# Attention with V as the stationary operand, two query blocks at a time, and outputs written feature-major

## What is computed

```python
def odd_mixer(h, w_qkv, ..., subln, w_o, rel_table, layer_idx):
    q, k, v = jnp.split(h @ w_qkv, 3, axis=-1)      # q, k: (b, s, H, 2, 64); v: (b, s, H, 128)
    ...
    def block(args):                                 # one block of 128 queries, all heads
        bias = rel_table[t5_bucket(kpos[None, :] - qpos[:, None])]
        sc = jnp.einsum('bqhmd,bkhmd->bhmqk', qi, k) * scale + bias[None, :, None]
        p = jax.nn.softmax(sc, axis=-1)
        a = p[:, :, 0] - lam * p[:, :, 1]
        return jnp.einsum('bhqk,bkhe->bqhe', a, v)
    ...
    o = rmsnorm(o, subln) * (1.0 - lam_init)
    return o.reshape(bsz, s, H * 2 * dh) @ w_o
```

## Time and profile before

| what | value |
|---|---|
| median of 3 runs | 2960.14 us (2956.94 to 2962.92) |
| the profiled execution, its own time | 2964.82 us |
| span of the profiled execution | 2963.0 us |
| TensorE busy | 2863.3 us, 97% |
| VectorE busy | 1922.0 us, 65% |
| ScalarE busy | 1197.6 us, 40% |
| attention, from the first scores of block 0 to the output projection | about 570 us of the span, 1578 to 2149 |

### The profile page before, as it was taken

The page is one execution under the profiler, slowest core; times in us unless marked ns, Lnnn a source line. Parts: engine busy times, 40 slices in busy tenths (PEclk is TensorE's granted clock), DMA queues, the critical chain, the costliest instruction groups (busy, mean ns, idle before and its releaser), DMA issues.

```text
span 2963.0 us, 34631 instructions
## 1 busy us (share of the span) xinstructions
PE 2863.3 (97%) x13481; PEld 2263.8 (76%) x13481; DVE 1922.0 (65%) x2488; ACT 1197.6 (40%) x1932; POOL 440.0 (15%) x322
## 2 busy tenths in 40 slices
PE   8999999999999999999998999999799999999999
PEld 6767776767768888877766888888676888887887
DVE  6548775655587666765667767766726966666254
ACT  2223327413243333433245565556624433334252
POOL 0420011261003222211000000000000222222010
PEclk7999999999999999999999999999899999999999
DMA  6334474016232222385550111111123222226453
GB/s 214 115 129 148 158 212 187 15 64 220 58 114 86 86 86 82 117 252 169 165 179 15 36 43 47 52 43 43 65 92 107 86 86 79 86 71 188 144 157 116
DMA packets 361688, 326.61 MB, mean 110 GB/s; under 512 B 11502, under 2 KB 319183, under 8 KB 361487
## 3 DMA queue, kind: packets, MB, share of 16 engines
q1 hardware_dynamic: 348486, 271.61, 29.4%
q0 software_dynamic: 12000, 48.61, 4.4%
q10 hardware_dynamic: 1040, 4.19, 0.4%
HBM read 263.88 MB, written 68.35 MB: 112 GB/s over the span
## 4 chain that ended last, share of the span: by engine, by line
PE 87%; DVE 7%; ACT 2%; DMA 2%; issue 1%; POOL 1%; SPq 0%; ACTq 0%; DVEq 0%; POOLq 0%
PE psum_gemm L1932 20%; PE psum_misc L1932 17%; PE psum_gemm L2378 8%; PE psum_gemm L216 6%; PE psum_gemm L217 6%; PE psum_gemm L220 6%; PE psum_misc L2442 3%; PE psum_gemm L2463 3%; PE psum_gemm L2451 3%; PE psum_misc L216 2%; PE psum_misc L217 2%; PE psum_misc L220 2%; DVE mix_out L285 1%; PE psum_gemm L318 1%; PE psum_misc L888 1%
## 5 line engine op out<-in xcount | busy, mean ns | idle before, releaser
L216 PE MATMUL psum_gemm<-h_hi,w_hi 128*128 128x512 f32 x816 | 330.3, 405 | 11.4 <-DVE h_lo L401 7.6
L217 PE MATMUL psum_gemm<-h_lo,w_hi 128*128 128x512 f32 x816 | 319.2, 391 | 0.0
L198 ACT ACTIVATE w_hi<-w_raw 128x1024 fp32r<-128x1024 f32 x93 | 97.8, 1055 | 453.8 <-PE psum_gemm L220 321.2
L1857 DVE TENSOR_TENSOR ring_lo<-piece_raw,ring_hi 128x512 fp32r<-128x512 f32 x192 | 136.0, 716 | 211.8 <-ACT ring_hi L1851 211.2
L220 PE MATMUL psum_gemm<-h_hi,w_lo 128*128 128x512 f32 x816 | 252.3, 390 | 0.0
L203 DVE TENSOR_TENSOR w_lo<-w_raw,w_hi 128x1024 fp32r<-128x1024 f32 x93 | 119.1, 1285 | 158.0 <-ACT w_hi L198 158.0
L1851 ACT ACTIVATE ring_hi<-piece_raw 128x512 fp32r<-128x512 f32 x192 | 112.7, 592 | 254.3 <-PE psum_misc L1932 213.8
L1932 PE MATMUL psum_misc<-h_hi,ring_hi 128*128 128x512 f32 x512 | 200.7, 392 | 1.2 <-DVE ring_lo L1857 1.1
L216 PEld LDWEIGHTS psum_gemm<-h_hi,w_hi 128*128 128x128 f32 x816 | 153.7, 188 | 61.5 <-issue 20.7
L1932 PE MATMUL psum_misc<-h_hi,ring_lo 128*128 128x512 f32 x512 | 199.4, 389 | 0.0
L1932 PE MATMUL psum_misc<-h_lo,ring_hi 128*128 128x512 f32 x512 | 199.2, 389 | 0.0
(11 more groups left out here) (415 smaller groups left out, 6830.9 us busy)
## 6 DMA issues: line engine op xcount, KB each, us to landing
ada_w<-in_w_ada SPq DMA_DIRECT2D x28, 1024.0 KB, 5.6
w_raw<-in_f_w_up SPq DMA_DIRECT2D x52, 512.0 KB, 4.8
ffn_act_scratch<-gate_act SPq DMA_DIRECT2D x42, 512.0 KB, 2.6
piece_raw<-in_f_w_down SPq DMA_DIRECT2D x80, 256.0 KB, 3.1
piece_raw<-ffn_act_scratch SPq DMA_DIRECT2D x80, 256.0 KB, 2.9
pair_raw<-in_f_w_up SPq DMA_DIRECT2D x36, 512.0 KB, 5.1
w_raw<-in_e_w_in SPq DMA_DIRECT2D x29, 512.0 KB, 4.6
x_scratch<-x_res SPq DMA_DIRECT2D x3, 4096.0 KB, 12.5
```

The lines of the kernel that those rows point to most:

```text
L198: act.activation(w_hi[:, s], w_raw[:, s], ACT.Copy).then_inc(s_hi, 1)
L216: pe.matmul(o, wh, rh[:, k, c], start=(k == 0), stop=False)
L217: pe.matmul(o, wh, rl[:, k, c], start=False, stop=False)
L1857: dve.tensor_tensor(Al[:, idx % 7, 0:n], src, Ah[:, idx % 7, 0:n].bitcast(F32), ALU.subtract).then_inc(s_wl, 1)
```

## The change

- Operands of the product with V change places. V is stationary and the map is moving; two query blocks stand side by side in `att_T`, so that one `av(p)` serves blocks 2p and 2p+1: per 128 keys three products of 256 columns (V hi with map hi, V hi with map lo, V lo with map hi). The output is feature-major, 128 features x 256 queries, and needs no transpose; `o_step`, `o_sum`, `o_part`, GpSimd's multiplication and the transposes ahead of the last head's part of the output projection go.
- Since the queries are now along the columns, a factor per query can't be applied while copying out. ScalarE scales the first map by one over its sum ahead of the combination (`scale`), VectorE computes the factors ahead of that (`factors`), and `combine` is left with the weighted sum.
- The sum of squares over the features is a product of the squares with a matrix of ones (`square_sums`, TensorE, 256 columns), between ScalarE's `o_evac` (copy and square) and `sums_copy`.
- The norm of a head works on 128 x 1024 numbers: a square root on ScalarE (`o_std`), and on VectorE a reciprocal and a multiplication (`o_norm`, at position 2 of the next head).
- The order: `av(p)` stands in even iterations between scores and transposes, `square_sums` in odd ones behind the transposes. The projections are dealt out as 12 in even and 24 in odd iterations, all at the iteration's end; at position 0, six of the 12 stand ahead of the transposes. A group's end is no longer put ahead of `av`.

```diff
--- before.py
+++ after.py
-            lo, hi = min(max(QM * (g + 1), 0), 144 * (ATT_HEADS - 1)), min(max(QM * (g + 2), 0), 144 * (ATT_HEADS - 1))
+            lo, hi = (min(36 * (i // 2) + 24 * (i % 2), 144 * (ATT_HEADS - 1)) for i in (g + 1, g + 2))
             cut = hi // 24 * 24
             return (lo, cut, hi, True) if cut > lo else (lo, hi, hi, False)
...
-                h, i = g // CH, g % 2
-                pe.wait_ge(s_aTl, g + 1)
+            def av(p):
+                h = p // QPAIRS
+                pe.wait_ge(s_aTl, 2 * p + 2)
                 pe.wait_ge(s_vl, h + 1)
-                if g >= 1:
-                    pe.wait_ge(s_on, g)
-                o = pG[:, 0, 256 * i:256 * i + 256]
+                if p >= 1:
+                    pe.wait_ge(s_omc, p)
                 for c in range(CH):
-                    pe.matmul(o, aT[:, i, 0, c], v_hl[:, h % 2, c], start=(c == 0), stop=False, skip_group_check=True)
-                    mm = pe.matmul(o[:, 0:P], aT[:, i, 1, c], v_hl[:, h % 2, c, 0], start=False, stop=(c == CH - 1),
-                                   skip_group_check=True)
+                    for x, (v, a) in enumerate(((0, 0), (0, 1), (1, 0))):
+                        mm = pe.matmul(pG[:, 0, 0:256], v_hl[:, h % 2, c, v], aT[:, a, c].rearrange("p s q -> p (s q)"),
+                                       start=(c == 0 and x == 0), stop=(c == CH - 1 and x == 2), skip_group_check=True)
                 mm.then_inc(s_av, 1)
+
+            def square_sums(p):
+                pe.wait_ge(s_on, p + 1)
+                if p >= 1:
+                    pe.wait_ge(s_omc, p)
+                pe.matmul(pG[:, 0, 256:512], ones[:], o_sq[:], start=True, stop=True, skip_group_check=True
+                          ).then_inc(s_oms, 1)
 
             def v_step(h):
...
@@ -2486,20 +2485,22 @@
                 lo, cut, hi, at_end = qkv_range(g)
                 if 0 <= g < NB - 2:
                     scores(g + 2)
+                if g >= 2 and g % 2 == 0:
+                    av(g // 2 - 1)
                 if g >= 0:
+                    if g % CH == 0 and g:
+                        first = min(lo + 6, hi)
+                        piece(lo, first)
+                        lo = first
                     pe.wait_ge(s_a, g + 1)
                     step(lambda c: E0[:, g % 3, c * P:(c + 1) * P], s_aT, s_aTl, g + 1)
-                if at_end:
-                    piece(lo, cut)
-                    lo = cut
-                if g >= 1:
-                    av(g - 1)
+                if g >= 3 and g % 2:
+                    square_sums((g - 3) // 2)
                 piece(lo, hi)
                 if g >= 0 and g % CH == CH - 1 and g + 1 < NB:
                     v_step((g + 1) // CH)
-                if g >= CH and g % CH == O_STEP:
-                    o_step(g // CH - 1)
-            av(NB - 1)
+            av(NQPAIR - 1)
+            square_sums(NQPAIR - 1)
 
         def att_act(act):
...
                                    ).then_inc(s_pe, 1)
 
+            def scale(g):
+                act.wait_ge(s_r, 2 * g + 2)
+                act.activation(E0[:, g % 3], E0[:, g % 3], ACT.Copy, scale=inv[:, g % 8, 0:1]).then_inc(s_asc, 1)
+
             def a_hi(g):
                 act.wait_ge(s_aT, g + 1)
                 if g >= 2:
-                    act.wait_ge(s_av, g - 1)
...
-                act.activation(junk[:], o_t[:, h % 2, b], ACT.Square, accum_out=o_ss[:, h % 2, b:b + 1]).then_inc(s_osq, 1)
+                    act.wait_ge(s_av, g // 2)
+                act.activation(aT[:, 0, :, g % 2], pG[:, 1].rearrange("p (c q) -> p c q", c=CH), ACT.Copy).then_inc(s_aTh, 1)
+
+            def o_evac(p):
+                h, i = p // QPAIRS, p % QPAIRS
+                act.wait_ge(s_av, p + 1)
+                if h and i == 0:
+                    act.wait_ge(s_of, h)
+                act.activation(o_f[:, 256 * i:256 * i + 256], pG[:, 0, 0:256], ACT.Copy)
+                if p >= 1:
+                    act.wait_ge(s_oms, p)
+                act.activation(o_sq[:], pG[:, 0, 0:256], ACT.Square).then_inc(s_on, 1)
+
+            def sums_copy(p):
+                h, i = p // QPAIRS, p % QPAIRS
+                act.wait_ge(s_oms, p + 1)
+                if h and i == 0:
+                    act.wait_ge(s_os, 16 * h)
+                act.activation(r_t[:, 256 * i:256 * i + 256], pG[:, 0, 256:512], ACT.Copy).then_inc(s_omc, 1)
 
             def o_std(h):
-                act.wait_ge(s_osq, CH * (h + 1))
-                act.activation(o_sd[:, h % 2], o_ss[:, h % 2], ACT.Sqrt, bias=eps[:, 0:1], scale=1.0 / P).then_inc(s_osd, 1)
+                act.wait_ge(s_omc, QPAIRS * (h + 1))
+                act.activation(r_t[:], r_t[:], ACT.Sqrt, bias=eps[:, 0:1], scale=1.0 / P).then_inc(s_osd, 1)
 
...
             probs(0)
             v_hi(0)
             probs(1)
+            scale(0)
             for g in range(-1, NB):
                 e = ended(g)
+                if 0 <= g < NB - 1:
+                    scale(g + 1)
                 if g >= 0:
                     a_hi(g)
                 if e and e[1] < 2:
                     kq_hi(*e)
                 elif e:
                     v_copy(e[0], e[2])
-                if g >= 2:
-                    o_square(g - 2)
-                if g >= 1:
-                    o_part(g - 1)
                 if 0 <= g < NB - 2:
                     probs(g + 2)
+                if g >= 2 and g % 2 == 0:
+                    o_evac(g // 2 - 1)
+                if g >= 3 and g % 2:
+                    sums_copy((g - 3) // 2)
                 if e and e[2]:
                     next_w(U_ATT + 3 * e[0] + e[1] + 2)
                 if g >= 0 and g % CH == CH - 1 and g + 1 < NB:
                     v_hi((g + 1) // CH)
-                if g >= CH and g % CH == O_STD:
+                if g > CH and g % CH == 1:
                     o_std(g // CH - 1)
-                if g >= CH and g % CH == O_STEP:
-                    o_copy(g // CH - 1)
                 if g > NB - CH:
                     o_hi(act, g - NB + CH - 1)
-            o_square(NB - 2)
-            o_part(NB - 1)
-            o_square(NB - 1)
...
+            def factors(g):
                 s8 = g % 8
                 dve.wait_ge(s_pe, 2 * g + 2)
                 dve.reciprocal(inv[:, s8], sums[:, s8]).then_inc(s_r, 1)
                 dve.wait_ge(s_r, 2 * g + 1)
-                dve.scalar_tensor_tensor(ratio[:, s8, 0:1], sums[:, s8, 0:1], nlam[:, 0:1], inv[:, s8, 1:2], ALU.mult,
-                                         ALU.mult).then_inc(s_r, 1)
-                dve.wait_ge(s_r, 2 * g + 2)
-                dve.scalar_tensor_tensor(E0[:, g % 3], E1[:, g % 2], ratio[:, s8, 0:1], E0[:, g % 3], ALU.mult, ALU.add
+                dve.tensor_tensor(ratio[:, s8, 0:1], nlam[:, 0:1], inv[:, s8, 1:2], ALU.mult).then_inc(s_r, 1)
+
+            def combine(g):
+                dve.wait_ge(s_asc, g + 1)
+                dve.scalar_tensor_tensor(E0[:, g % 3], E1[:, g % 2], ratio[:, g % 8, 0:1], E0[:, g % 3], ALU.mult, ALU.add
                                          ).then_inc(s_a, 1)
...
+            def o_norm(h):
                 dve.wait_ge(s_osd, h + 1)
-                dve.reciprocal(o_rs[:, h % 2], o_sd[:, h % 2]).then_inc(s_ors, 1)
+                dve.reciprocal(r_t[:], r_t[:]).then_inc(s_ors, 1)
+                dve.wait_ge(s_ors, h + 1)
+                dve.scalar_tensor_tensor(r_t[:], o_f[:], nlam[:, 4:5], r_t[:], ALU.mult, ALU.mult).then_inc(s_of, 1)
...
                 e = ended(g)
+                if 0 <= g < NB - 1:
+                    factors(g + 1)
...
                     combine(g + 1)
-                if g >= 1:
-                    o_sum(g - 1)
                 if e and e[2]:
                     split_lo(dve, U_ATT + 3 * e[0] + e[1] + 2)
                 if g >= 0 and g % CH == CH - 1 and g + 1 < NB:
                     v_lo((g + 1) // CH)
-                if g >= CH and g % CH == O_STD:
-                    o_rstd(g // CH - 1)
+                if g > CH and g % CH == 2:
+                    o_norm(g // CH - 1)
```

86 lines of the change are left out of this document (23 added, 63 removed).

## The result

| | before | after |
|---|---|---|
| median of the runs | 2958.5 us (2955.6 to 2962.9) | 3065.2 us (3063.5 to 3076.0) |
| profiled execution's span | 2963.0 us | 3061.8 us |
| mean granted clock in it | 0.982 | 0.972 |

The ratio is 1.0368, 95% interval 1.0355 to 1.0381: 3.7% slower. The forecast of 3063 is 2 us off.

A forecast was written before the change was run, and what follows sets the result against it. TensorE's queue bounds seven heads, a loop through VectorE and ScalarE the last. Six heads at 13.9 (83), the first 5, the last 15: 103 us on 2964.8 gives 3068, less 4.7 is 3063; its own range 3030 to 3095, overall 2990 to 3095.

The forecast's parts named there:

- a: Positions 1 and 5: the next group waits for the shared bank's copy, 1.6 for k, 0.9 for v; 2.5 us.
- b: Position 4: `av` waits for `sums_copy` of position 3, behind the copy and `probs`; 2.0 us.
- c: Position 7: `square_sums` waits for `o_evac`, behind the copy and `probs` of position 6; 1.5 us.
- d: Position 3: the transposes wait for `combine`, behind the low part in VectorE's queue; 1.2 us.
- e: Positions 0 and 1: `av` waits 0.7 for `sums_copy`, the transposes of position 1 wait 0.8 for `combine`; 1.5 us.
- f: Position 3: `square_sums`, ahead of 24 projections, waits for `o_evac`, which waits for `o_norm` (reciprocal 6.6 us); 8.0 us.
- g: TensorE at 1.2 GHz for a while behind the long wait of f; 1.7 us, from 0 to twice that.
- TensorE's queue: Saving per head from fewer products with V, no output transposes, fewer changes of form and V's split covered; 4.5 us.
- Rival 3: The reciprocal runs at VectorE's other rate, 1.3 us, so f is 2.7 and g 0; 3010 us; chance 0.08.
- rival 4: Only the large wait counts, the small ones are covered by unseen slack; 2997 us; chance 0.15.
- Rival 5: `scale` isn't hidden on ScalarE, or 1.2 GHz costs more after 8 us; 3090 us and above; chance 0.11.
- rival 2: TensorE's queue alone decides, each of seven heads gains 4.5 us; 2929 us; chance 0.04.

The follow-up runs named there:

- small: Changed kernel, output and sums copied earlier on ScalarE, `combine` ahead of the low part, groups of positions 1 and 5 ahead of the transposes: 3020.6 us.
- final2: `final` with VectorE's `o_lo` one iteration later in the last head's blocks: 2948.1 us, ratio 0.9962 to before.
- lnexp: Changed kernel with VectorE's reciprocal replaced by a logarithm and an exponential on ScalarE in place of the root, orders unchanged: 3006.5 us.
- final: `small` with the edit of `lnexp`, `o_evac` early at every position and `o_norm` ahead of the low part of the transposed map: 2954.3 us.
- no_recip: Changed kernel with VectorE's reciprocal of 128x1024 left out, so the output differs: 3009.1 us, ratio 1.0169 to before.
- act_order: Changed kernel with `o_evac` (but at position 2) and `sums_copy` ahead of the group's copy and `probs` on ScalarE: 3050.5 us.
- sq_late: Changed kernel with the product with ones behind the 24 projections of its iteration, reciprocal kept: 3032.1 us, ratio 1.0246 to before.

## Why the prediction was right, step by step

Per head, forecast and then what the trace of after shows:

| | forecast | measured |
|---|---|---|
| a | 2.5 | (9.0 + 4.1) / 6 = 2.2 |
| b | 2.0 | 1.7 |
| c | 1.5 | 0.9 |
| d | 1.2 | 1.0 |
| e | 1.5 | 0.8 + 0.6 = 1.4 |
| f | 8.0 | 7.4 |
| g | 1.7 | 2.1 |
| TensorE's queue | -4.5 | -2.2, by difference |
| sum | 13.9 | 14.5 |

The rows for b, c and e, TensorE in order of time:

```profile
1707.06 3.11 PE L2460 MATMUL psum_gemm<-att_T,v_split 128*128 128x256 f32 x24 [1.72 <-ACT o_factor_T L2555]
...
1735.10 0.70 PE L2468 MATMUL psum_gemm<-o_squares,ones 128*128 128x256 f32 x2 [0.88 <-ACT o_squares L2548]
```
```profile
1744.60 3.11 PE L2460 MATMUL psum_gemm<-att_T,v_split 128*128 128x256 f32 x24 [0.81 <-ACT o_factor_T L2555]
...
1753.55 1.09 PE L2448 MATMUL psum_gemm<-ident,probs_a 128*128 128x128 f32 x8 [0.61 <-DVE probs_a L2644]
```

**What was right for its reason.** Each wait came at the place, for the tile and for the engine that the three queues had given. All but g are somewhat shorter than worked out, by 0.1 to 0.6 us. One reason is in the trace: the two operations of `o_evac` took 0.66 us together (1781.05 to 1781.71) where 0.9 was counted. The reciprocal took 6.547 us where 6.56 was worked out from its two narrower rows. Rival 3 hung on it and fell with that row, rival 4 on the walk through the queues, and fell with `small`, which took a to e away and gave 7.8 us a head. Rival 5 is out for the six heads: g came to 2.1, within its bounds, and no wait in them is outside a to f. Against rival 2 the forecast said that a reciprocal alone on any row costs more than 0.9 us; the row of 8 columns has 0.2. What holds is that every rate it considered gives more than 0.9 at 1024 columns. Had I gone by the reading of the Trainium skill's page "VectorE: DVE Perf Modes" (section on the fixed hardware budget) as eight cycles a column, f would have been 10.0 by that estimate; the measured 6.25 ns are six cycles at 0.96 GHz, and the rows were the better guide.

**What was mis-sized: TensorE's saving.** I had put 4.5 us and the head shows about 2.2. This is the term of the sum that was wrong. One `av` of after, and what follows it:

```profile
1724.83 3.14 PE L2460 MATMUL psum_gemm<-att_T,v_split 128*128 128x256 f32 x24
1727.81 1.04 PE L2448 MATMUL psum_gemm<-ident,probs_a 128*128 128x128 f32 x8
```

24 start to start take 2.98 us, 0.124 each and not 0.115, four times a head 0.9 us. Half the price of 512 columns was too low: eight transposes of 128 columns take 0.85 us, 0.106 each, 256 columns 0.124 and 512 columns 0.229, so the price isn't in proportion to the columns. The product with ones costs 0.49 and not 0.24:

```profile
1715.31 1.09 PE L2448 MATMUL psum_gemm<-ident,probs_a 128*128 128x128 f32 x8
1716.24 0.60 PE L2468 MATMUL psum_gemm<-o_squares,ones 128*128 128x256 f32 x2
1716.49 0.58 PE L2375 MATMUL psum_gemm<-h_hi,w_hi 128*128 128x512 f32 x1
1716.90 0.40 PE L2375 MATMUL psum_gemm<-h_lo,w_hi 128*128 128x512 f32 x1
```

From the transposes' start to the second projection's is 1.59 us, and 1.10 where no such product stands between (1711.11 - 1710.01 in the same trace). The trace holds two records for each of these products, whose operands the kernel keeps as fp32 and not as fp32r like those of its other products. I had halved the interval of the earlier trace rows as two products, and 0.49 lies outside even its bound of 0.3. That is another 4 x 0.25 = 1.0. Together 1.9 of the 2.3 us are explained. The 0.4 left is as large as the term for fewer changes of form, for which the forecast had no row; no run here shows that term. In `final2`, where no long wait blurs it, a head gains 1.95 us of products and 0.9 of the old wait, and has 1.0 of waits left. So rival 2, TensorE's queue alone, would have been worth 7 x 2.85 = 20 us, some 2940 and not 2929, with every wait covered.

So the sum was right in part by luck, because errors met: the waits and the clock 1.7 us a head too long (18.4 for 16.7), the saving 2.3 too large; and over the whole, 87.3 for 83, 2.0 for 5, 17.5 for 15, and -6.7 upstream, where the program is the same, so that this is a difference between two executions. The forecast's own range was also narrower than its words: a to e at half or one and a half and g at its bounds, all at once, give 3021 to 3105 and not 3030 to 3095.

**The end of the last head.** Here the chain of 13.5 us for 13.2 came out. The last head's part starts 13.55 us behind the first product of the output projection (2262.23 - 2248.68), and before it was 13.2:

```profile
2262.23 0.50 PE L216 MATMUL psum_misc<-h_hi,w_hi 128*128 128x512 f32 x1 [3.63 <-DVE h_lo L2755]
```

So the reciprocal has a price here too that the comparison with before hides: without it this wait is gone, and all behind the attention takes 810.0 us (`lnexp`, `final`) in place of 813.1 (816.2 in `small`). Of the 58.6 us that `lnexp` saves, the traces of after and `lnexp` show 52.6 in the six heads, 3.2 in the last one and 3.1 here.

**The last head.** The sum was 2.5 us short, but its parts don't stand. I had given 7.9 + 1.7 of the 15 us to `o_norm` and the clock behind it, and without the reciprocal the last head is only 4.0 shorter (72.7; 73.5 in `lnexp`). TensorE's waits in it are 18.9 us before and 35.3 after; `neg_max` has 8.1 of these against 2.5, and `o_lo` accounts for 3.6 us of time. The granted clock there is 0.76 against 0.86, 0.75 in `no_recip` and 0.79 in `final2`. The orders of `act_order` and `small` made it 2.8 and 2.5 us longer. Since `scale` and `o_evac` are in all variants, what of the remaining 8 us in `final2` is their place in the loop and what is the clock was not told apart. It stays open.

## What to carry to other kernels

Before giving a strictly ordered queue a new instruction that waits, ask what stands behind it: here 24 projections waited for a norm that they don't need. Price a wide operation by the narrow rows of the same operation and not by its neighbours of the same width. A smaller count of matmuls was worth 2 us a head, the order around them 7.8 and one slow operation 8.8; if an exchange of operands seems to lose, mend the order and the slow operation before judging it.

## What the runs showed of the hardware that I had not expected

- VectorE's fp32 reciprocal is linear in the columns: 202 ns for 8, 1755 for 256, 6547 for 1024, five times the 1285 ns of a weighted sum of the same width. A logarithm and an exponential on ScalarE (1.15 and 1.06 us) with the multiplication left on VectorE take its place: ScalarE's busy time of a head rises by 1.0 us (49.3 to 50.3 in `lnexp`), and the kernel takes 3006.5 us, no more than the 3009.1 with no reciprocal at all.
- After 7.4 us without work TensorE ran at a granted clock of 0.50 for a while and lost 2.1 us in the mean. Short waits were no protection: the same waits, none above 1.7 us, left heads of `no_recip` at 1.00 four times and at 0.98 and 0.95 once each (these two 1.5 us longer). With 2.0 us as the longest wait the six heads of `sq_late` had 0.93 to 0.96. In `final2`, with 0.5 us as the longest, five heads had 1.00.
- A product of 128x256 with fp32 operands appears as two records and costs about as much as four of the 24 (0.49 against 4 x 0.124).
